# Moving weight buffers, activations and arena to other start addresses in SBUF

## The reference

```python
# first block, each of two layers; h has 256 tokens, hc 256 context tokens
h  = h  + 0.5 * g1 * swiglu(modulate(rms_norm(h,  norm_ffn1), sh1, sc1), w_gate, w_up, w_down)    # 1024 -> 2816 -> 1024
hc = hc + 0.5 * cg1 * swiglu(...)                     # the same weights, other modulation
p  = modulate(rms_norm(h, norm_mix), shm, scm) @ w_in   # queries, keys, values of 16 heads
h  = h + gm * (attention(p) @ w_out)                    # window, global and neighbourhood heads
h  = h + 0.5 * g2 * swiglu(..., w_ffn2_gate, w_ffn2_up, w_ffn2_down)
# second block, one layer
p  = rmsnorm(x, norm_mix) @ w_in                      # rwkv, mla, diff attention and gates
x  = x + (sum of three gated branches) @ w_o
x  = x + conv_ffn(rmsnorm(x, norm_ffn), w_up, w_down)
return rmsnorm(x, norm_final)
```

## Time and profile before

| what | us |
|---|---|
| median of 3 runs (2408.27 to 2413.86) | 2413.43 |
| the profiled execution | 2415.45 |
| its span, first to last instruction | 2414.1 |
| TensorE matmuls busy | 2291.4 (95%) |
| VectorE busy | 1497.1 (62%) |
| ScalarE busy | 967.4 (40%) |
| GpSimd busy | 363.1 (15%) |

### The profile page before, as it was taken

The page is one execution under the profiler, slowest core; times in us unless marked ns, Lnnn a source line. Parts: engine busy times, 40 slices in busy tenths (PEclk is TensorE's granted clock), DMA queues, the critical chain, the costliest instruction groups (busy, mean ns, idle before and its releaser), DMA issues. The chain is left out here.

```text
span 2414.1 us, 37082 instructions
## 1 busy us (share of the span) xinstructions
PE 2291.4 (95%) x14376; PEld 1934.1 (80%) x14376; DVE 1497.1 (62%) x2305; ACT 967.4 (40%) x1546; POOL 363.1 (15%) x365
## 2 busy tenths in 40 slices
PE   6999999998999999999999989889999998998998
PEld 4888887665678888878888866579998996898998
DVE  4666766455676666676663364566667746676774
ACT  4222223455442222242222245444446334556763
POOL 1000001000000000000000010069992762000000
PEclk7999999999999999999999999989998998999999
DMA  6554444111134444434442241125453221243444
GB/s 274 188 185 180 174 169 151 70 36 53 62 123 177 176 175 170 156 137 158 177 179 99 101 128 53 53 91 188 170 197 119 91 101 65 91 158 140 167 160 143
DMA packets 52615, 331.05 MB, mean 137 GB/s; under 512 B 6544, under 2 KB 7824, under 8 KB 21648
## 3 DMA queue, kind: packets, MB, share of 16 engines
q1 hardware_dynamic: 49040, 319.15, 36.6%
q0 software_dynamic: 3456, 10.25, 1.4%
HBM read 325.56 MB, written 3.80 MB: 136 GB/s over the span
## 5 line engine op out<-in xcount | busy, mean ns | idle before, releaser
L1173 PE MATMUL bank<-u_hi,whi 128*128 128x512 f32 (+1 forms) x2512 | 869.9, 346 | 41.5 <-DVE wlo L568 15.6
L1174 PE MATMUL bank<-u_lo,whi 128*128 128x512 f32 (+1 forms) x2512 | 853.2, 340 | 0.0
L1175 PE MATMUL bank<-u_hi,wlo 128*128 128x512 f32 (+1 forms) x2512 | 852.6, 339 | 0.0
L568 DVE TENSOR_TENSOR wlo<-raw,whi 128x2048 fp32r<-128x2048 f32 (+2 forms) x208 | 434.5, 2089 | 299.1 <-ACT whi L566 298.9
L1173 PEld LDWEIGHTS bank<-u_hi,whi 128*128 128x128 f32 x2512 | 481.1, 192 | 119.8 <-issue 38.0
L1175 PEld LDWEIGHTS bank<-u_hi,wlo 128*128 128x128 f32 x2512 | 481.0, 191 | 51.8
L1174 PEld LDWEIGHTS bank<-u_lo,whi 128*128 128x128 f32 x2512 | 481.2, 192 | 49.7 <-issue 0.2
L566 ACT ACTIVATE whi<-raw 128x2048 fp32r<-128x2048 f32 (+2 forms) x208 | 355.2, 1708 | 326.8 <-PE bank L1175 232.9
L1235 ACT ACTIVATE sil<-bank 128x512 f32<-128x512 f32 (+1 forms) x88 | 47.8, 544 | 543.6 <-PE bank L1175 543.5
L1173 PE MATMUL bank<-hidden_hi,whi 128*128 128x512 f32 x528 | 205.4, 389 | 0.0
L1174 PE MATMUL bank<-hidden_lo,whi 128*128 128x512 f32 x528 | 205.4, 389 | 0.0
(11 more groups left out here) (427 smaller groups left out, 2950.9 us busy)
## 6 DMA issues: line engine op xcount, KB each, us to landing
raw<-in_stream SPq DMA_DIRECT2D x231, 1024.0 KB, 4.8
raw<-in_stream SPq DMA_DIRECT2D x80, 704.0 KB, 4.0
first_ada<-in_stream SPq DMA_DIRECT2D x8, 1024.0 KB, 16.9
raw<-in_stream SPq DMA_DIRECT2D x8, 768.0 KB, 4.3
skew<-rpb_rows POOLq DMA_DIRECT2D x8, 336.0 KB, 6.2
nbr_bias<-skew POOLq DMA_DIRECT2D x24, 112.0 KB, 3.6
h<-in_tokens SPq DMA_DIRECT2D x1, 2048.0 KB, 12.0
uq_ukv<-in_small POOLq DMA_DIRECT2D x1, 1536.0 KB, 8.1
```

The source lines that it names most:

```text
L568: v.tensor_tensor(self.lo[to][:, 0:n], raw[:, 0:n], self.hi[to][:, 0:n].bitcast(F32), ALU.subtract).then_inc(self.s_lo, 1)
L1173: pe.q.matmul(dst, w[0], x[0], start=start, stop=False)
L1174: pe.q.matmul(dst, w[0], x[1], start=False, stop=False)
L1175: return pe.q.matmul(dst, w[1], x[0], start=False, stop=stop)
```

## The change

Every number in this section is an address of the built program. The second pair of weight buffers is allocated behind the first, with the small table `mod_a` and 32 bytes between; `mod_g` and 64 bytes come between it and h; and 64 bytes of gap stand before the arena, whose start is no longer aligned to h. No instruction is added, removed or moved on any engine; each engine's order of instructions, tiles and waits is the same as before. Buffers allocated behind the arena move with it.

```diff
     raw = [sb(f"raw{i}", [P, SLAB]) for i in range(2)]
-    whi = [sb(f"whi{i}", [P, SLAB], F32R) for i in range(2)]
-    wlo = [sb(f"wlo{i}", [P, SLAB], F32R) for i in range(2)]
+    whi, wlo = [None] * 2, [None] * 2
+    whi[0], wlo[0] = sb("whi0", [P, SLAB], F32R), sb("wlo0", [P, SLAB], F32R)
+    mod_a = sb("mod_a", [P, L1, 3, 2, KC])
+    sb("gap_0", [P, 8])
+    whi[1], wlo[1] = sb("whi1", [P, SLAB], F32R), sb("wlo1", [P, SLAB], F32R)
+    mod_g = sb("mod_g", [P, L1, 3, 2, KC])
+    sb("gap_1", [P, 16])
     H_AT = (nc.sbuf_base + 31) // 32 * 32
...
-    mod_a = sb("mod_a", [P, L1, 3, 2, KC])
-    mod_g = sb("mod_g", [P, L1, 3, 2, KC])
     arena_size = FC * T * 4 * 2
-    ARENA_AT = nc.sbuf_base + (H_AT - nc.sbuf_base) % 512
-    sb("arena_gap", [P, (ARENA_AT - nc.sbuf_base) // 4])
+    sb("gap_2", [P, 16])
+    ARENA_AT = (nc.sbuf_base + 31) // 32 * 32
     sb("arena", [P, arena_size // 4])
```

## The result

The changed kernel takes 2456.28 us, the median of three runs (2454.68 to 2456.87), against 2413.43: a ratio of 1.0187, 95% interval 1.017 to 1.0204. It is 42.85 us slower. The profiled execution took 2456.87 us, with a span of 2455.5. Its mean granted clock was 0.975 against 0.972 in the one before, so the clock explains none of the loss.

A forecast was written before the change was run, and what follows sets the result against it. The prediction took TensorE's matmul rate as the bound; -15.9 - 5.7 - 2.0 - 2.9 - 1.5 summed to -28.0 us, for a forecast of 2386 us against a median of 2413.43, range 2362 to 2445.

The forecast's parts named there:

- What bounds the kernel: Whole kernel: bound by how fast TensorE takes one matmul after another; its matmuls are busy 95% of the span.
- (a): 512-column matmuls in stages where TensorE does not stop, 4752 in all: faster, -15.9 us for pair 1, -5.7 for pair 0.
- (b): The other 512-wide matmuls, 864 interleaved with attention: 4.55 ns less each, half on the path, -2.0 us.
- (c): 4560 256-column matmuls that lay 64 ahead: pair 1 +5.5 us, pair 0 -9.8, leaving -2.9 us after waits.
- (d): 672 256-column matmuls that lay 0 or 256 ahead (y, branches, queries): half of the gain on the path, -1.5 us.
- (e): The rest: VectorE and ScalarE show no sensitivity to where they start, DMA's load targets stay; cost 0.
- Half a unit: Rival in TensorE's streams: starting at 32 modulo 64 touches one unit more, 6.7 ns a matmul; +24.2 us, 2438; chance 0.31.
- Wide streams at their floor: Rival: 512-column streams are already at their best, so (a) and (b) are 0; -4.4 us, 2409.0; chance 0.18.
- the addresses do nothing: Rival: differences between TensorE's steps are states into which it falls at a restart; 2413.4 us; chance 0.09.
- two reads meet: In TensorE's matmuls, loading the next tile meets the stream that runs meanwhile; 512-wide ones lose 13.3 ns, 32 columns, each.

The follow-up runs named there:

- The fine map: Bare matmuls alone, rest of the kernel before left out: weights at home 0, 512 and 256 columns, distances 0 to 252 in steps of 4 bytes; 2087.07 us.
- the map: Bare matmuls alone, rest of the kernel before left out: 512 and 256 columns, weights' homes 0, 32, 128, 160, distances 0 to 480 by 32; 1768.82 us.
- the widths map: Bare matmuls alone, rest of the kernel before left out: weights at home 0, widths 512, 384, 256, 128, distances 0 to 240 by 16; 819.63 us.

## Why the prediction was wrong

**What bounds the kernel** was right: the waits kept their size, no instruction moved, and nearly all of the 42.85 us are in the steps of `three`.

**(a) is the step that failed.** It priced the new distances of the 512-wide streams with differences between 256-wide steps, and 96 by its nearest neighbour, 64: -6.7 ns at 64 behind, -2.4 ns at 96. Both signs were wrong. A 512-wide stream at 0 ahead loses 32 columns, and so does a 256-wide one, which made them look like one rule; but for 512 columns 32 is the lowest of all distances tried, while for 256 it is one of the two dearest in steps of 32 bytes. The new distances, 96 and 192 modulo 256, cost 48 columns: 233.3 - 226.7 = 6.6 ns more, and 4752 x 6.6 = +31.4 us instead of -21.6. The fine map shows that the nearest distance is no guide either, since neighbours differ widely. The row that came closest was the 233 ns behind the clock's rise, which I had as the upper bound of pair 0 alone.

**(b)** has the same fault: 864 x 6.6 = +5.7 us at most, instead of -2.0. The run with activations and arena alone moved, whose 5616 wide matmuls would give 37.1 by this price and which measured 37.2, suggests that the share hidden behind waits is small; its interval, 30 to 41 us, leaves room for a few us of it.

**(c)** was right for pair 1, whose new distance a row of the same width had: it went to 120.0 ns as predicted (+2.2 ns x 2280 = +5.0 us). Pair 0, priced like 64 behind at 113.5, takes 117.5 (-0.3 ns x 2280 = -0.7 us). Instead of -2.9 it is about +4 if none of it is hidden behind waits.

**(d)** pair 1, at 192 or 448, went to about 114 ns as taken; pair 0, at 96, stayed at 120: 336 x -6.7 = -2.3 us at most, against -1.5.

**The sum** by measured steps is 31.4 + 5.7 + 4.3 - 2.3 = +39.1 us, against 41.4 in the span and 42.85 in the medians. The 39.1 is an estimate from the measured steps and the counts. The 2 to 4 us that are left are within the spread of the kernel before between executions (2408.27 to 2413.86), and I leave them unassigned.

**(e)** held: L568 2337 ns, DVE 1495.2 us and ACT 967.3 busy against 1497.1 and 967.4, at their operands' new starts. Its reading of the earlier trace rows was weak, though: 2355 / 2048 is 1.15 ns an element and 685 / 512 is 1.34, which is not one rate.

**The rivals.** Half a unit named the right side, and its observable (under 1006 in the window) came true, but its mechanism is false: the map shows no effect of the weights' home on 512-wide steps, and the kernel with everything at 160 loses nothing. Wide streams at their floor had half of the truth: 226.7 ns is the lowest 512-wide step, but not one that the other distances keep. That the addresses do nothing is refuted by two steps in one stage, 233.3 and 226.7 ns, with the second pair alone moved. What the Trainium skill concludes from two independent read ports ("TensorE: Matmul & The Clock Gate", section "Step-by-step: what each phase is for"), that loading the next tile takes nothing from the running stream, therefore doesn't describe these float32 triples at the upper clock: where the tiles lie changes the stream's step by 6.6 ns. The Trainium skill's section "Back-to-back issue gap" on the same page gives N / 2.4 + 2.5 ns as the gap of an isolated warm matmul, by which a 512-wide step would be an estimated 215.8 ns; no settled 512-wide step in these runs was below 226.7.

**What stays open.** The prediction said that two reads meet. Whether reads collide, which ones, and why the price is jagged, no run here shows; I have only the total of a step. The lower clock, at which the loss is gone in both kernels, narrows it to something that comes up at the upper rate. Nor is it settled what chooses between 16 and 27 columns at one and the same distance of a 256-wide stream. And the maps keep both weight buffers at one home and both stream buffers at one home; triples whose own buffers differ weren't measured alone (y_lo is such a case, with few matmuls).

## What to carry to other kernels

A price read at one shape holds for that shape: that two widths lose the same 32 columns at one distance said nothing on how they lose at another. Where a kernel runs matmul behind matmul with a new weight tile for each, read the step against the width at the granted clock, and before moving buffers measure the few distances in question, at the widths in question, with a kernel of bare matmuls: its settled 512-wide steps were those of the whole kernel to a fraction of a nanosecond (226.7, 228.9 and 233.3 ns). For float32 streams of 512 columns, weights and streams at equal starts modulo 256 were best here; for 256 columns 112 bytes ahead was, and was worth 0.23%.

## What the runs showed of the hardware

- A matmul's step in such triples, at the granted clock of 1.00, depends on (start of the stream - start of the weight tile) modulo 256 bytes; at 512 columns neither start alone changes it: 226.7 to 234.3 ns at 512 columns and distances in steps of 32, 113.3 to 120.2 at 256 columns.
- The loss at distance 0 is 32 columns at 512, 384 and 256 columns; at the 15 other distances of the widths map it is larger at 512 columns than at 256 (at 64: 26.6, 32 and 37.4 columns at 256, 384 and 512).
- At the lower clock there is no loss at 512 columns: about 426 ns a step at distance 0 and, in the changed kernel, at 352 or 448.
- Streams of 128 columns take 111.7 ns at every distance, nearly as long as the best 256-wide ones.
- At some distances of 256-wide streams (64 and 192) the same code settles at 113.3 ns in one panel and at 117.8 in another.
- VectorE and ScalarE took the same time within 1% at the starts tried: L568 2355 ns before and 2337 after, and ScalarE was busy 967.4 and 967.3 us.
